# Hybrid decoder step with PEER experts on one Trainium2 core: bias rows laid by GpSimd, first weights in quarters, the query norm's weights at the evacuation, first head's experts in two passes of eight

## What is computed

```python
def mixer_inputs(xn, pos, w_in, g_q, w_uq, g_kv, w_uk):
    c_q, c_kv, k_r, q_b, k_b, v_b, q_i, k_i, w_i = jnp.split(xn @ w_in, cuts, axis=-1)
    c_q = rmsnorm(c_q, g_q)
    q = (c_q @ w_uq).reshape(b, s, MLA_HEADS, MLA_NOPE + MLA_ROPE)
    ...
    c_kv = rmsnorm(c_kv, g_kv)

def dsa_attend(q, k_sel, v_sel, s_sel, qpos, rel_bias):
    bias = rel_bias[rel_bucket(dist)]          # T5 relative bias, 32 buckets, 8 heads
    ...

def peer_ffn(x, w_pq, sub_keys, u_emb, v_emb):
    q = (xc @ w_pq).reshape(c, PEER_HEADS, 2, PEER_HALF)
    s = jnp.einsum('chpd,hpkd->chpk', q, sub_keys)
    sv, si = lax.top_k(s, 16)                  # 16 of 128 keys, both halves, 8 heads
    cand = sv[:, :, 0, :, None] + sv[:, :, 1, None, :]
    cv, ci = lax.top_k(cand, 16)               # 16 experts of 16384 for each token and head
    ...
    act = gelu(einsum('chkd,cd->chk', u_emb[eid], xc))
    return einsum('chk,chkd->cd', softmax(cv) * act, v_emb[eid])
```

## Time and profile before

| | us |
|---|---|
| median of 3 runs (1009.95, 1010.02, 1011.06) | 1010.02 |
| the profiled execution | 1012.5 |
| its span, first to last instruction | 1010.6 |
| TensorE busy | 730.6 (72%) |
| VectorE busy | 689.6 (68%) |
| ScalarE busy | 402.4 (40%) |
| GpSimd busy | 619.0 (61%) |
| HBM read and written | 377.90 MB and 3.88 MB |

### The profile page before, as it was taken

How to read it: one execution, slowest core, us unless ns; L and a number is a source line. 1 busy time by engine, 2 the same in 40 slices (tenths; PEclk the granted TensorE clock), 3 DMA queues, 4 the chain that set the end, 5 groups by cost and what they waited for, 6 DMA issues and landing times.

```text
span 1010.6 us, 13868 instructions
## 1 busy us (share of the span) xinstructions
PE 730.6 (72%) x4233; PEld 373.1 (37%) x4233; DVE 689.6 (68%) x1729; ACT 402.4 (40%) x1152; POOL 619.0 (61%) x584
## 2 busy tenths in 40 slices
PE   8899979575888878966668676767496577564444
PEld 3477636241454535733213322323132244221101
DVE  2272955998597654599987499999964354666542
ACT  1163232332655671233315353654356343242422
POOL 0000474777777776466777767667777466677771
PEclk9999999787999889988859989779767788798555
DMA  9943599999999999999999999999999999999996
GB/s 346 329 161 137 195 392 379 403 414 408 411 397 382 391 412 405 410 400 385 356 375 387 406 407 407 406 405 404 410 404 407 411 415 419 411 409 409 406 409 262
DMA packets 122907, 381.01 MB, mean 377 GB/s; under 512 B 16106, under 2 KB 40762, under 8 KB 118226
## 3 DMA queue, kind: packets, MB, share of 16 engines
q0 software_dynamic: 83696, 304.81, 76.8%
q1 hardware_dynamic: 39042, 75.26, 20.0%
q10 hardware_dynamic: 96, 0.07, 0.0%
HBM read 377.90 MB, written 3.88 MB: 378 GB/s over the span
## 4 chain that ended last, share of the span: by engine, by line
DVE 28%; DMA 26%; PE 19%; POOL 14%; issue 7%; SPq 4%; ACT 2%; POOLq 0%; DVEq 0%
DMA rows<-in_peer_v,eid 13%; PE bank L471 12%; POOL rows L2021 6%; DVE rows L1477 6%; PE acc L471 6%; POOL rows L2039 5%; DMA rows<-in_peer_u,eid 3%; DMA wring<-in_w_in 3%; DMA x<-in_peer_u,eid 3%; DVE ql_t L1786 3%; DVE small L1785 2%; SPq L2112 2%; DMA more_u<-in_peer_u,eid 2%; DMA z<-in_cache_kv 2%; DVE more_u L1477 1%
## 5 line engine op out<-in xcount | busy, mean ns | idle before, releaser
L471 PE MATMUL acc<-rows,spread 128*64 128x512 f32 (+1 forms) x1124 | 328.0, 704 | 150.6 <-DMA rows<-in_peer_v,eid 121.5
L2021 POOL DMA_INDIRECT rows<-in_peer_v,eid x254 | 272.6, 1073 | 100.9 <-issue 70.1
L2039 POOL DMA_INDIRECT rows<-in_peer_u,eid x184 | 192.4, 1045 | 82.9 <-issue 47.8
L471 PEld LDWEIGHTS acc<-rows,spread 128*64 128x64 f32 (+1 forms) x1124 | 84.2, 156 | 319.3 <-issue 242.4
L1477 DVE CUSTOM_DVE_ANT_0 rows<-rows,xr_even 128x1024 f32<-128x1024 f32 x89 | 108.4, 1219 | 45.7 <-DMA rows<-in_peer_u,eid 44.8
L1477 DVE CUSTOM_DVE_ANT_0 rows<-rows,xr_odd 128x1024 f32<-128x1024 f32 x95 | 116.1, 1222 | 31.5 <-DMA rows<-in_peer_u,eid 31.0
L2039 POOL DMA_INDIRECT first_u<-in_peer_u,eid x37 | 40.9, 1106 | 104.2 <-DVE eid L1872 76.2
L1121 ACT ACTIVATE spread<-wide_consts,wts 128x64 f32<-128x64 f32 (+1 forms) x288 | 83.7, 338 | 4.7
L471 PE MATMUL acc<-more_v,spread 128*64 128x512 f32 (+1 forms) x140 | 69.2, 687 | 19.2 <-DMA rows<-in_peer_v,eid 12.6
L1112 ACT ACTIVATE gelus<-dots 128x2 f32<-128x2 f32 x144 | 28.6, 199 | 116.6 <-DVE dots L1477 116.1
L1114 ACT ACTIVATE wts<-gelus,gate 128x1 f32<-128x1 f32 x288 | 69.1, 287 | 4.7
(11 more groups left out here) (285 smaller groups left out, 1195.4 us busy)
## 6 DMA issues: line engine op xcount, KB each, us to landing
wring<-in_w_pq SPq DMA_DIRECT2D x12, 1024.0 KB, 8.8
z<-in_w_pq SPq DMA_DIRECT2D x5, 1024.0 KB, 7.8
wring<-in_cache_ckv SPq DMA_DIRECT2D x40, 128.0 KB, 11.7
rows<-in_w_in SPq DMA_DIRECT2D x2, 2048.0 KB, 14.9
wring<-in_w_pq SPq DMA_DIRECT2D x2, 2048.0 KB, 12.2
wring<-in_w_out SPq DMA_DIRECT2D x4, 1024.0 KB, 10.1
wring<-in_cache_kv SPq DMA_DIRECT2D x32, 128.0 KB
rows<-in_peer_v,eid POOLq DMA_INDIRECT x254, 12.2
```

Of the source, the lines that this page charges most:

```text
L471: return T.matmul(o, lhsT=l, rhs=r, start=start, stop=stop, skip_group_check=True)
L2021: nc.gpsimd.indirect_dma_start(out=v_ring[V_PLACE[n]], out_offset=None, in_=inp["peer_v"], in_offset=bass.IndirectOffsetOnAxis(ap=eid[t][: ...
L2039: nc.gpsimd.indirect_dma_start(out=u_ring[U_PLACE[n]], out_offset=None, in_=inp["peer_u"], in_offset=bass.IndirectOffsetOnAxis(ap=eid[t][: ...
```

## The change

Six things are done, in five places.

1. **Bias rows.** The product with `hot` is gone from TensorE, and so are its three evacuations on ScalarE and the load of `hot` (144.5 KB). `rel_bias` comes transposed (8 x 32), and GpSimd lays the 1156 columns of the bias row itself with 32 copies, one for each run of equal buckets (915 columns the longest, 129 the next, 15 of one column). The HBM to HBM spreading of the prompt's strip waits until `w_in` block 3 has landed.
2. **First weights.** The first half of `w_in` block 0 comes in two quarters, with a semaphore each. TensorE starts on the identity, VectorE on `g_attn`, with no common wait.
3. **Norm weights.** `g_q` comes as three columns (1.5 KB, before: broadcast to 128 partitions, 192 KB) and is multiplied in when ScalarE evacuates the transposed `c_q`, in three activations in the place of one. The rope table and `g_kv` move behind `w_in` block 3, and `latents(0)`, which needs them, runs after `copies(0)`.
4. **w_uq** has a semaphore of its own.
5. **First head in two passes.** `first_choice` takes the 8 best keys of each half, makes 72 candidates of them, chooses 8 experts, works out their numbers and signals slots 0 to 7; then come the second eight keys, the other 64 candidates, the second 8 experts and the second signal. `STARTS[0]` has slot 8 as a further start, and GpSimd waits for its signal there.
6. **TensorE's sums.** Two of the six `advance` calls in front of the query product of heads 2 and 3 (`query_product(1, 0)`) are made inside it, behind its first and its second quarter.

```diff
+STARTS[0].insert(1, 8)
+GIVEN = [sum(len(p) for p in STARTS[:t]) for t in range(3)]
...
             def z_product(t, c):
                 if c == 0:
-                    pe.wait_ge(w_in_half, 16)
+                    pe.wait_ge(w_in_quarter, 16)
...
                 for k in range(8):
+                    if (c, k) == (0, 2):
+                        pe.wait_ge(w_in_half, 16)
...
+                    if (c, t) == (1, 0) and q < 2:
+                        experts.advance(CHOOSE)
...
-                    for i in range((6, 2, 4, 6)[c] if t == 0 else 0):
+                    for i in range((4, 2, 4, 6)[c] if t == 0 else 0):
                         experts.advance(CHOOSE)
...
             def cq_evac(t):
                 n = P[t]
                 b = ready(act, ("cq", t))
-                copy(("cq", t), cq_t[:, :, 0:n], split(b[:, 0:3 * n], 3, n))
+                if t == 0:
+                    act.wait_ge(g_q_in, 16)
+                for j in range(3):
+                    copy(("cq", t), cq_t[:, j, 0:n], b[:, j * n:(j + 1) * n], j == 2, g_q[:, j:j + 1])
...
+            def first_choice():
+                b = ready(dve, ("sc", "a", 0))
+                score = [b[:, 128 * j:128 * j + 128] for j in range(2)]
+                keys = [sc[:, j, :] for j in range(2)]
+                for j in range(2):
+                    i = V.max(sv[:, j, 0:8], score[j])
+                link(V, i)
+                for j in range(2):
+                    i = V.max_index(si_u[:, j, 0:8], sv[:, j, 0:8], score[j])
+                V.tensor_tensor(first_cand[:, 0:8], free(sv[:, 0, 0:1], (0, 8)), sv[:, 1, 0:8], ALU.add)
+                link(V, V.tensor_tensor(first_cand[:, 16:72].rearrange("p (a b) -> p a b", b=8), free(sv[:, 0, 1:2], (1, 7), (0, 8)),
+                                        free(sv[:, 1, 0:1], (0, 7), (1, 8)), ALU.add))
+                pick_eight(0, 72)
+                locate(0, 8)
+                V.match_replace(out=first_cand[:, 0:72], in_to_replace=cv[:, 0, 0:8], in_values=first_cand[:, 0:72], imm_value=TAKEN)
...
+                pick_eight(8, STAIR)
+                V.tensor_tensor(gt[:, 0, :], cv[:, 0, :], free(cv[:, 0, 0:1], (0, PTOP)), ALU.subtract).then_inc(gate_sub, 1)
+                locate(8, 16)
+                share_gates(0, 0)
...
-            read_done(pool, ("bias", 2))
+            pool.wait_ge(rel_in, 16)
+            for b, first, n in bucket_runs():
+                i = nc.gpsimd.tensor_copy(bias_row[:, first:first + n], free(rel_t[:, b:b + 1], (0, n)))
+            i.then_inc(bias_row_ready, 1)
+            pool.wait_ge(bias_row_ready, 1)
             nc.gpsimd.dma_start(scr_b, bias_row).then_inc(bias_row_out, 16)
...
+            pool.wait_ge(lodge_in[3], 16)
             nc.gpsimd.dma_start(scr_d, bass.AP(scr_b.tensor, GU - 384, [[0, 128], [GU, NH], [1, WD]])).then_inc(scr_d_out, 16)
...
-                    load(lodge[0][:, 0:2048], inp["w_in"][:, 0:2048], w_in_half)
+                    load(lodge[0][:, 0:1024], inp["w_in"][:, 0:1024], w_in_quarter)
+                    load(lodge[0][:, 1024:2048], inp["w_in"][:, 1024:2048], w_in_half)
...
-            load(relb, inp["rel_bias"], hot_in)
-            load(hot_u, cst["hot"], hot_in)
...
-            for o, i in norm_consts:
-                load(o, i, norm_in)
+            load(g_q[:, :], inp["g_q"], g_q_in)
             lodge_columns("in", 3)
+            load(w_uq[:, :, :], inp["w_uq"], w_uq_in)
             for o, i in post_consts:
                 load(o, i, post_in)
```

More of the change, by code:

```diff
@@ L103, in free, with bucket_runs @@
     return bass.AP(ap.tensor, ap.offset, [list(ap.ap[0])] + [list(d) for d in dims])
+def bucket_runs():
+    dist = np.maximum(PAST + NT - 1 - np.arange(GU), 0)
+    nf = np.maximum(dist, 1).astype(np.float32)
+    large = 16 + (np.log(nf / np.float32(16)) / np.float32(math.log(8.0)) * np.float32(16)).astype(np.int32)
+    bucket = np.where(dist < 16, dist, np.minimum(large, REL_B - 1))
+    runs = []
+    for j, b in enumerate(bucket.tolist()):
+        if runs and runs[-1][0] == b:
+            runs[-1][2] += 1
+        else:
+            runs.append([b, j, 1])
+    return runs
 def build(nc, inp, cst, out, scr_b, scr_d, scr_s, scr_z2):
@@ L477, in _ @@
         def _(pe):
-            def bias_rows():
-                pe.wait_ge(hot_in, HOT_IN)
-                for c in range(3):
-                    w = min(512, GU - 512 * c)
-                    b = take(pe, ("bias", c))
-                    full(mm(b[0:NH, 0:w], relb, hot_u[:, c * 512:c * 512 + w]), ("bias", c))
             def z_product(t, c):
                 if c == 0:
-                    pe.wait_ge(w_in_half, 16)
+                    pe.wait_ge(w_in_quarter, 16)
                     w = lodge_view(lodge[0], "in", 0)
@@ L1027, in _ @@
                     transpose_x(c, "x")
+            pe.wait_ge(w_uq_in, 16)
             pe.wait_ge(post_in, POST_IN)
@@ L1085, in copy @@
                     drained(c, name)
-            def bias_rows():
-                for c in range(3):
-                    w = min(512, GU - 512 * c)
-                    b = ready(act, ("bias", c))
-                    copy(("bias", c), bias_row[:, c * 512:c * 512 + w], b[0:NH, 0:w])
             def keep_z1(c):
@@ L1571, in post @@
                     norms(t)
+                    latents(t)
                 link(V, rope(t, zt[0:n, O_KI:O_KI + 1], 1, 32, kk[0:n, 0:1], 32))
@@ L1874, in choose, with share_gates @@
                 i.then_inc(slots_ready, 1)
+                share_gates(t, p)
+                pause()
+            def share_gates(t, p):
+                n, (h0, m) = 128, PARTS[t][p]
+                hs = slice(h0, h0 + m)
                 dve.wait_ge(gate_exp, CHOSEN[t] + p + 1)
@@ new lines, in pick_eight, with locate @@
+            def pick_eight(first, w):
+                k = slice(first, first + 8)
+                link(V, V.max(cv[:, 0, k], first_cand[:, 0:w]))
+                link(V, V.max_index(ci[:, 0, k], cv[:, 0, k], first_cand[:, 0:w]))
+            def locate(first, m):
+                k = slice(first, first + 8)
+                for half, step in enumerate((1024.0, 128.0)):
+                    V.scalar_tensor_tensor(out=placed[:, half, 0:m], in0=iota16[:, 0:m], scalar=step, in1=si_u[:, half, 0:m],
+                                           op0=ALU.mult, op1=ALU.add)
+                link(V, V.tensor_scalar(pa[:, 0, k], ci[:, 0, k], 0x1F8, 7, ALU.bitwise_and, ALU.logical_shift_left))
+                V.scalar_tensor_tensor(out=pb[:, 0, k], in0=pa[:, 0, k], scalar=2048.0, in1=pa[:, 0, k], op0=ALU.is_ge, op1=ALU.mult)
+                link(V, V.tensor_scalar(pa[:, 0, k], pa[:, 0, k], 1024.0, 0.0, ALU.subtract, ALU.max))
+                link(V, V.scalar_tensor_tensor(out=pb[:, 0, k], in0=ci[:, 0, k], scalar=128.0, in1=pb[:, 0, k], op0=ALU.mult, op1=ALU.subtract))
+                for half, (place, e) in enumerate(((pa, ea), (pb, eb))):
+                    o = first_hot[:, 128 * half:128 * half + 8 * m].rearrange("p (k c) -> p k c", c=m)
+                    link(V, V.tensor_tensor(o, free(place[:, 0, first:first + 1], (1, 8), (0, m)),
+                                            free(placed[:, half, 0:1], (0, 8), (1, m)), ALU.bitwise_xor))
+                    link(V, V.tensor_reduce(out=e[:, k], in_=o, axis=AX.X, op=ALU.min))
+                for j, q in SPREAD[0]:
+                    i = V.scalar_tensor_tensor(out=eid[0][WIDE * q:WIDE * q + WIDE, first + j:first + 8:PAIR],
+                                               in0=ea[WIDE * j:WIDE * j + WIDE, first + q:first + 8:PAIR], scalar=float(KEYS),
+                                               in1=eb[WIDE * j:WIDE * j + WIDE, first + q:first + 8:PAIR], op0=ALU.mult, op1=ALU.add)
+                i.then_inc(slots_ready, 1)
@@ L1929, in _ @@
             link(V, copies(0))
+            dve.wait_ge(post_in, POST_IN)
+            latents(0)
             for t in tiles:
```

66 lines of the change are left out of this document (37 added, 29 removed).

## The result

The changed kernel takes **1016.81 us** (median of 4 runs, 1016.22 to 1017.48); the kernel before 1010.36 in the same series. The ratio is 1.0067, 95% interval 1.0054 to 1.008. The forecast was 1001.9 us. Yet the first 110 us came out close to the forecast.

What follows compares the result with a forecast made beforehand. From 126 us on, gathers keep the DMA engines full, so an earlier start ends the program equally earlier. Terms of 4.5, 2.2 and 1.4 sum to 8.1 us, from the median 1010.02 to 1001.9 us; range 999.0 to 1006.5.

Steps and rivals of the forecast that it cites:

- Term 1: Start: z of tile 0 ends 5.1 us earlier, cut by the wait for stored cache rows to 4.5 us (3.3 to 5.8).
- Term 2: First gather: head 0's two-pass choice sends it 3.8 us earlier; u slot 6 limits the gain to 2.2 us (1.5 to 3.8).
- Term 3: GpSimd's pause before 171.60: an earlier query product frees it before the DMA engines run dry, 1.4 us (0.5 to 1.8).
- B: Rival: GpSimd's 32 copies make the bias late for VectorE; slower by 5.5 us, about 1015.5; chance 0.06.
- the bias strip: HBM to HBM spreading, issue to `bias_in`: 30.4 us from 27, ending at 57.5, 9 us before the bias is needed.
- D: Rival: later stages hold the gathers elsewhere and the early lead melts to within 2 us, about 1009; chance 0.06.
- A: Rival: early part held elsewhere (low clock through z block 0, or stores no earlier than 60); gain 3 to 5.3; chance 0.19.
- The two rules weighed: Queue turns would cut Term 1 to 3.3 us, sum 6.9; VectorE and GpSimd exclusion would delay TensorE 1.4 us, sum 7.3.

Runs made afterwards that it cites:

- e2: The changed kernel with the tile of `g_q` as wide as before (1536 bytes), so every SBUF tile has its old address; 1003.8 us, ratio 0.993.
- e3: The changed kernel with the constant `hot` kept in HBM as an input, SBUF tiles as in the change; 1014.7 us, ratio 1.0035.
- f1: The changed kernel with 480 unused bytes ahead of `wring`: page tiles start as before the change modulo 512, gather tiles and `bias_d` do not; 1002.4 us.
- f2: The changed kernel with gather tiles and `bias_d` starting as before the change modulo 512, page tiles 32 bytes off; 1016.8 us, ratio 1.0074.
- h1: The changed kernel with tiles at multiples of 512, without the two-pass choice and the new order of sums; 992.9 us, ratio 0.9807.
- g1: The kernel before with all tiles that take gathers or pages at multiples of 512 bytes, nothing else changed; 999.3 us, ratio 0.9882.
- h2: The changed kernel with tiles at multiples of 512 and ScalarE's own DMA queue issuing the five stores of tile 0's cache rows; 990.5 us, ratio 0.9794.
- f4: The changed kernel with three spacers, so every tile that takes gathers or pages starts at a multiple of 512 bytes; 993.7 us, ratio 0.9855.
- e1: The changed kernel with the tile of `g_q` 44 bytes wide instead of 12, moving every tile behind it up 32 bytes; 1014.3 us, ratio 1.004.

## Why the prediction was wrong

**The step that failed** is in the first paragraph: "A gather that starts a microsecond earlier ends the program a microsecond earlier, as long as the DMA engines stay fed." They stayed fed; the share from 600 to 640 us is 1.04 before and after. What did not stay is the time of a packet. The sum had no term for the line that makes the tile of `g_q` smaller, which moved every tile behind it by an odd multiple of 32 bytes. That term measured 11 to 14 us: 13.8 by the ratios of e2 and the changed kernel (0.993 and 1.0067), 10.9 by e2 and e3 in one session (1003.8 and 1014.7), 14.3 by f1 and f2 in another (1002.4 and 1016.8).

**Without it the total holds.** e2's ratio of 0.993 times 1010.02 is 1002.9 us, for a forecast of 1001.9 and a range of 999.0 to 1006.5. That each term by itself reaches the end in the median is not shown: h1, the start alone, is as fast as the whole change.

**Term 1** (4.5 forecast): the choice begins 4.8 us earlier. But its steps erred in both directions. z of tile 0 ended 9.1 us earlier and not 5.1: the z product began at 7.88 as forecast (7.9), but TensorE's clock rose sooner, and 32 passes of blocks 0 and 1 took 15.49 us. The weight loads stand 0.85 us apart until 10.60 and 0.43 from 11.19 on, where the forecast took 16.5:

```profile
10.60 0.34 PEld L489 LDWEIGHTS bank<-rows,xt 128*128 128x128 f32 x1 [0.52 <-issue]
11.19 0.19 PEld L489 LDWEIGHTS bank<-rows,xt 128*128 128x128 f32 x1 [0.25 <-issue]
11.62 0.19 PEld L489 LDWEIGHTS bank<-rows,xt 128*128 128x128 f32 x1 [0.24 <-issue]
```

The stores landed at 58.3, not 59.5, and the table load that the forecast put behind them ran ahead of them, at 51.62. So the first exponential came 7.2 us earlier (58.4 against 65.65), not 4.5. From there to the choice 2.4 us were lost again, by the low clock. Right by luck in this run, and 6 to 8 us in others (g1's 101.7, or the earlier trace rows, against 95.1 to 96.0).

**Term 2** (2.2, bounds 1.5 to 3.8): 1.6 at 220 us. The first pass took 4.55 us for 4.7 forecast, and u slots 2 and 6 were released by TensorE as said. **Term 3** (1.4, bounds 0.5 to 1.8): 2.1 at 220 us, above its bounds. The pause is 4.64 us and not under 2, but the DMA share from 160 to 180 us is 1.02 and the rate 412 GB/s.

**The rivals.** B's condition was not met: 5.83 us for 32 copies is 0.18 each, `bias_d` has landed at 56.6, and VectorE's use of the bias at 63.59 waits for nothing. (The forecast's 30.4 us for the bias strip counts the issue of 0.93 us twice; it was 29.5, and nothing hangs on it.) D's sign came true ("some 8 us ahead at 200 us and not at 900"), by another mechanism: nothing held the gathers at a place. A's low clock came, but later, at 62 to 70 us. The chance of 0.06 for slower held only mechanisms within the engines' order; that memory addresses move with a tile's size was in none of them.

**The two rules weighed.** With the stores on a queue of their own (h2) they landed no earlier, but their packets did go in turn with those of two fuller queues: 95 of 288 from 50 to 52 us. With the Trainium skill's rule that queues take turns packet by packet ("DMA: Bandwidth & Descriptors", Queues, rings and completion order) this trace agrees. The forecast's reading of it, that the stores would gain nothing but the 0.33 MB (0.8 us), did not come true: SP's load behind them went out at 58.36 against 60.67. The mean square of x took 1.74 us beside GpSimd's copies against 1.23 before, and VectorE's transposes were ready half a microsecond later than before (7.8 against 7.4 us), which is the 7.88 of TensorE's start. With the Trainium skill's rule that such instructions exclude each other ("SBUF — State Buffer", two separate sides) this agrees, at a third of the 1.4 us estimated. The list of instructions shows both sides of it: the copy of 915 columns ran from 4.41 to 5.35 us (0.94), the mean square from 4.69 to 6.43, and the next copy, of only 14 columns, from 5.31 to 6.48, 1.17 us where the median copy takes 0.18.

## What to carry to other kernels

Where a kernel is bound by transfers, print the start addresses of the tiles before and after every edit; a smaller tile moves all behind it, and here 32 bytes cost 1.1%, and a start at a multiple of 256 for all DMA targets gave 1.2%. When a lead melts at an unchanged DMA share, divide share by packets in a stretch with and one without the second stream, and see that the mix of packet sizes is the same: if the packet's time moved, look at addresses and not at waits. Judge an edit against the kernel before with its tiles held in place (g1 against f4), or its address effect is taken for its merit.

## What the runs showed of the hardware

- The gathers' packets of 4096 bytes, alone from 900 to 940 us, take 163.1 to 163.3 ns into tiles 64, 96, 128 or 192 bytes off a multiple of 256 (before, changed, e1, f3), and 159.7 into tiles at one (f4): 409 against 418 GB/s. How far off the tile starts made no difference.
- Pages loaded into tiles that start 32, 64 or 128 bytes off a multiple of 256 slow the gathers beside them: 407 GB/s in the kernel before, 393 to 395 in the changed one, e1 and f3 from 600 to 640 us, all at a share of 1.04.
- An idle time of TensorE of 2.10 us was followed by a granted clock of 0.51 and 0.63 (62 to 66 and 66 to 70 us), one of 1.24 us (h1) by 0.59 and 0.99, those of 1.05 us or less by 1.00.
- Packets of a lightly filled queue go in turn with those of two fuller ones: 95 of 288 in 2 us (h2, 50 to 52 us).
